# First modulation of a diffusion trunk by quarters of the channels, with the norm's squares summed on TensorE

## What is computed

```python
m = silu(c) @ ada_w + ada_b          # (6 * 1024,) for c, and again for c_ctx
sh1, sc1, g1, sh2, sc2, g2 = split(m, 6)
h = x * rsqrt(mean(x * x, channels) + 1e-6) * norm1_g
h = h * (1 + sc1) + sh1              # latents by c, context by c_ctx
q, i_in, gate, zf = h @ hg_w_in      # projections of the HGRN2 mixer
```

## Time and profile before

| what | us |
|---|---|
| median of 3 timed executions | 1887.09 |
| lowest and highest of them | 1884.05, 1888.6 |
| the profiled execution | 1884.44 |
| its span, first to last instruction | 1882.6 |
| TensorE busy in the span | 1794.5 |
| VectorE busy | 1160.9 |
| ScalarE busy | 676.3 |
| GpSimd busy | 79.3 |

### The profile page before, as it was taken

How to read it: one execution, slowest core, us unless ns; L and a number is a source line. 1 busy time by engine, 2 the same in 40 slices (tenths; PEclk the granted TensorE clock), 3 DMA queues, 4 the chain that set the end, 5 groups by cost and what they waited for, 6 DMA issues and landing times.

```text
span 1882.6 us, 31499 instructions
## 1 busy us (share of the span) xinstructions
PE 1794.5 (95%) x13510; PEld 1533.7 (81%) x13510; DVE 1160.9 (62%) x1921; ACT 676.3 (36%) x999; POOL 79.3 (4%) x146
## 2 busy tenths in 40 slices
PE   4999999999878999999999999999899999999997
PEld 4999999999766888888888888878655878888885
DVE  4467668666874676524564265576554598487485
ACT  4334333443222333312322133333776344233242
POOL 0000000000300000000000000000343000000000
PEclk9999999999988999999999999999999999999998
DMA  7221222112201033223332232222000222232222
GB/s 299 101 90 51 86 91 91 68 69 91 79 2 56 34 124 112 95 108 112 114 121 102 90 118 107 79 71 79 24 1 1 89 90 90 101 101 91 99 95 106
DMA packets 45801, 166.16 MB, mean 88 GB/s; under 512 B 4960, under 2 KB 5344, under 8 KB 45664
## 3 DMA queue, kind: packets, MB, share of 16 engines
q1 hardware_dynamic: 45664, 164.16, 24.4%
HBM read 162.05 MB, written 2.10 MB: 87 GB/s over the span
## 4 chain that ended last, share of the span: by engine, by line
PE 88%; DVE 7%; ACT 2%; issue 1%; DMA 1%; POOL 0%; DVEq 0%; SPq 0%; ACTq 0%
PE slot L437 31%; PE slot L426 9%; PE slot L428 8%; PE slot L427 8%; PE slot L884 4%; PE slot L886 4%; PE slot L885 4%; PE MB L494 2%; PE MA L886 2%; PE MA L884 2%; PE MA L885 2%; PE MA L598 2%; PE slot L837 2%; PE MB L804 1%; PE slot L814 1%
## 5 line engine op out<-in xcount | busy, mean ns | idle before, releaser
L1316 DVE TENSOR_TENSOR WL<-WR,WH 128x1024 fp32r<-128x1024 f32 x204 | 249.4, 1223 | 229.0 <-ACT WH L939 228.0
L939 ACT ACTIVATE WH<-WR 128x1024 fp32r<-128x1024 f32 x204 | 215.4, 1056 | 388.6 <-DMA WR<-in_w 388.6
L426 PE MATMUL slot<-HH,WH 128*128 128x384 f32 (+2 forms) x848 | 304.1, 359 | 16.8 <-DVE HL L1475 6.2
L428 PE MATMUL slot<-HH,WL 128*128 128x384 f32 (+2 forms) x848 | 293.8, 346 | 0.0
L427 PE MATMUL slot<-HL,WH 128*128 128x384 f32 (+2 forms) x848 | 293.6, 346 | 0.0
L437 PE MATMUL slot<-HH,WH 128*128 128x256 f32 (+1 forms) x816 | 212.2, 342 | 2.5 <-DVE ACC L1685 1.6
L437 PE MATMUL slot<-HH,WL 128*128 128x256 f32 (+1 forms) x816 | 210.1, 339 | 0.0
L437 PE MATMUL slot<-HL,WH 128*128 128x256 f32 (+1 forms) x816 | 207.7, 336 | 0.0
L426 PEld LDWEIGHTS slot<-HH,WH 128*128 128x128 f32 x848 | 161.3, 190 | 37.1 <-issue 10.3
L437 PEld LDWEIGHTS slot<-HH,WH 128*128 128x128 f32 x816 | 151.6, 189 | 25.8 <-issue 7.1
L437 PEld LDWEIGHTS slot<-HL,WH 128*128 128x128 f32 x816 | 153.8, 188 | 18.0
(11 more groups left out here) (234 smaller groups left out, 2950.5 us busy)
## 6 DMA issues: line engine op xcount, KB each, us to landing
WR<-in_w SPq DMA_DIRECT2D x204, 512.0 KB, 3.5
ada_raw<-in_ada SPq DMA_DIRECT2D x80, 512.0 KB, 4.6
AD<-in_ada SPq DMA_DIRECT2D x6, 1024.0 KB, 18.0
X<-in_x SPq DMA_DIRECT2D x4, 768.0 KB, 8.4
ada_raw<-in_ada SPq DMA_DIRECT2D x2, 1024.0 KB, 13.0
out<-Y SPq DMA_DIRECT2D x8, 256.0 KB, 2.2
Y<-in_masks SPq DMA_DIRECT2D x1, 512.0 KB, 17.7
rope<-in_rope SPq DMA_DIRECT2D x1, 512.0 KB, 3.8
```

Of the source, the lines that this page charges most:

```text
L426: mm(SLOT[s][:, po], WH[w % NB][:, k, :], hi[:, k, to], start=(k == 0), stop=False)
L428: last = mm(SLOT[s][:, po], WL[w % NB][:, k, :], hi[:, k, to], start=False, stop=(k == kn - 1))
L939: go(WH[t % NB][:, :, :], WR[t % NB][:, :, :], ACT.Copy).then_inc(w_hi_done, 1)
L1316: tt(WL[t % NB][:, :, :], WR[t % NB][:, :, :], WH[t % NB][:, :, :].bitcast(F32), ALU.subtract).then_inc(w_split, 1)
```

## The change

The first four groups are replaced by four quarters: quarter q holds the shift and the scale of channels 2q and 2q+1, 256 columns of each. Each quarter is loaded by four transfers of 512 KB, whose rows in memory are 256 values (1 KB) long instead of 1024 (4 KB). Weight tiles 0 and 1 come behind quarter 0, and tile 2 is issued ahead of the masks. `quarter(q)` on VectorE adds the bias and makes the coefficients of two channels at once.

The squares are no longer added on VectorE. ScalarE writes them to four buffers, and TensorE sums each channel's on arrival, 48 one-column products in all. The Sqrt table is brought in after channel 1's square. Fillers (`keep_busy`) are put ahead of the sums, between them, around the spread and around the first turn: 7, then 1 seven times, 3, 8, 1 and 7. TensorE's list has the quarters' products between the steps of the first two tiles. GpSimd makes the low half of weight tile 0, and VectorE that of tile 1 after waiting for it; VectorE made both before. ScalarE makes the high halves of both tiles between rows 0 and 1.

```diff
             for i in range(4):
                 sp.dma_start(X[:, 2 * i:2 * i + 2, :], x_in[:, 2 * i:2 * i + 2, :]).then_inc(x_in_done[i], 16)
-            for g in range(ADA_FIRST):
-                at = 4 * ADA_ORDER[g]
-                for k in (0, 2):
-                    dst = AR0[:, k:k + 2, :, :] if g == 0 else AD0[:, 4 * g - 4 + k:4 * g - 2 + k, :, :]
-                    sp.dma_start(dst, ada_in[at + k:at + k + 2].rearrange("n p (f o) -> p n f o", f=2)).then_inc(ada0_in[2 * g + k // 2], 16)
-                if g == 1:
+            for q in range(ADA_FIRST):
+                for f in range(2):
+                    g = 2 * f + q // 2
+                    at = (q % 2) * 256
+                    for k in range(2):
+                        cols = ada_in[4 * g:4 * g + 4].rearrange("n p o -> p n o")[:, :, 512 * k + at:512 * k + at + 256]
+                        sp.dma_start(first_weights(q)[:, f, :, k, :], cols).then_inc(ada0_in[q], 16)
+                if q == 0:
                     for t in range(2):
                         sp.dma_start(WR[t][:, :, :], w_in[t]).then_inc(w_in_done[t], 16)
+            sp.dma_start(WR[2][:, :, :], w_in[2]).then_inc(w_in_done[2], 16)
             sp.dma_start(mask_stage, masks_in).then_inc(masks_in_done, 16)
...
+            def weights_low(t):
+                pool.wait_ge(w_hi_done, t + 1)
+                pool.tensor_tensor(WL[t % NB][:, :, :], WR[t % NB][:, :, :], WH[t % NB][:, :, :].bitcast(F32), ALU.subtract).then_inc(w_split, 1)
+
+            weights_low(0)
             split_heads()
...
+            pe.wait_ge(small_in_done, 16)
+            pe.wait_ge(ident_in_done, 16)
+            REST = SLOT[1][:, 512:768]
+            keep_busy(7, REST)
             pe.wait_ge(silu_ready, 1)
...
-            square_sums(0)
+            squares.add(KC)
+            for k in range(KC):
+                pe.wait_ge(sq_ready, k + 1)
+                for c in range(NCH):
+                    last = mm(MA[:, c:c + 1], SQ4[k % 4][:, c * P:(c + 1) * P], ones[:, :], start=(k == 0 and c == 0), stop=(k == KC - 1 and c == NCH - 1))
+                last.then_inc(sq_summed if k < KC - 1 else ss_ready, 1)
+                if k < KC - 1:
+                    keep_busy(1, REST)
+            stats.add()
+            keep_busy(3, REST)
+            spread(0, MA)
+            keep_busy(8, REST)
             ada_first(0)
-            pe.wait_ge(ident_in_done, 16)
+            keep_busy(1, REST)
             ada_turn()
-            spread(0, MA)
-            ada_first(1)
-            ada_turn()
-            ada_first(2)
+            keep_busy(7, REST)
...
             first_steps(0)
+            ada_first(1)
+            first_steps(1, (0,))
             ada_turn()
-            first_steps(1)
+            first_steps(1, (1,))
+            ada_first(2)
+            first_steps(2, (0,))
+            ada_turn()
+            first_steps(2, (1,))
+            first_steps(3)
             ada_first(3)
-            first_steps(2)
+            first_steps(4, (0,))
             ada_turn()
-            for k in range(3, KC):
+            first_steps(4, (1,))
+            for k in range(5, KC):
                 first_steps(k)
...
-                square(c, slice(0, TOK))
-            added.add(KC - 2)
+                if c >= 4:
+                    act.wait_ge(sq_summed, c - 3)
+                go(SQ4[c % 4], X[:, c, :], ACT.Square).then_inc(sq_ready, 1)
+                if c == 1:
+                    go(sqrt_set[:, :], eps_t[:, :], ACT.Sqrt)
...
             row_copy(0)
+            split_high(1)
+            first_his(0, 2)
             row_copy(1)
-            split_high(1)
-            first_his(0, 1)
+            first_his(2, 3)
             row_copy(2)
-            first_his(1, 3)
+            first_his(3, 5)
             row_copy(3)
-            first_his(3, 4)
+            first_his(5, KC)
             split_high(2)
-            first_his(4, KC)
...
+            def first_low():
+                low.add()
+                dve.wait_ge(w_split, 1)
+                split_low(1)
...
-                coefs(0)
+                quarter(0)
                 dve.wait_ge(rstd_spread, stats.now())
                 scaled(0)
-                split_low(0)
                 scaled(1)
                 low(0)
-                split_low(1)
+                first_low()
+                low(1)
+                quarter(1)
                 scaled(2)
-                low(1)
...
```

More of the change, by code:

```diff
@@ L61 @@
 ADA_FIRST = 4
-ADA_ORDER = (0, 2, 1, 3)
 NB = 3
@@ L208, in trunk @@
         SSQ = Y[:, 2, :]
+        SQ4 = [Y[:, i, :] for i in (0, 1, 2, 5)]
         NT = [Y[:, 3, :], Y[:, 4, :]]
@@ L215, in trunk @@
         ident_in_done, masks_in_done = sem("ident_in_done"), sem("masks_in_done")
-        ada0_in = [sem(f"ada0_in{i}") for i in range(2 * ADA_FIRST)]
+        ada0_in = [sem(f"ada0_in{i}") for i in range(ADA_FIRST)]
         ada0_used = sem("ada0_used")
@@ L226, in trunk @@
         ada_copied, ada_turned, ada_ready = sem("ada_copied"), sem("ada_turned"), sem("ada_ready")
-        sq_ready, sq_added = sem("sq_ready"), sem("sq_added")
+        sq_ready, sq_added, sq_summed = sem("sq_ready"), sem("sq_added"), sem("sq_summed")
         ss_ready, std_ready = sem("ss_ready"), sem("std_ready")
@@ L253, in ada_row, with first_weights @@
             return row0 if n < ADA_FIRST else RB if n < ADA_FIRST + HEADS else row2
+        def first_weights(q):
+            part = AR0[:, :, :, :] if q == 0 else AD0[:, 4 * q - 4:4 * q, :, :]
+            return part.rearrange("p a b o -> p (a b o)").rearrange("p (f n k o) -> p f n k o", f=2, n=4, k=2)
         def of_level(t, at, tokens, s):
@@ L348, in load_piece @@
                 sp.dma_start(AR[i % 4][:, :, :], ada_in[n].rearrange("p (f o) -> p f o", f=2)).then_inc(piece_in[i % 4], 16)
-            for t in range(2, TILES):
-                if t >= NB:
-                    sp.wait_ge(tile_done, t - NB + 1)
+            for t in range(NB, TILES):
+                sp.wait_ge(tile_done, t - NB + 1)
                 sp.dma_start(WR[t % NB][:, :, :], w_in[t]).then_inc(w_in_done[t % NB], 16)
@@ L535, in spread, with keep_busy @@
                 last.then_inc(rstd_spread, 1)
-            def keep_busy(n):
+            def keep_busy(n, dst=MA[:, 512:768]):
                 for _ in range(n):
-                    mm(MA[:, 512:768], ident[:, :], small[:, 0:256], start=True, stop=True)
+                    mm(dst, ident[:, :], small[:, 0:256], start=True, stop=True)
             def norm_pe(first, more=True):
@@ L551, in norm_pe, with ada_first @@
                     keep_busy(7)
+            pe.wait_ge(small_in_done, 16)
+            pe.wait_ge(ident_in_done, 16)
+            REST = SLOT[1][:, 512:768]
+            keep_busy(7, REST)
             pe.wait_ge(silu_ready, 1)
[L554 to L559, removed]
+            def ada_first(q):
+                pe.wait_ge(ada0_in[q], 64)
+                for c in range(KC):
+                    for m in range(4):
+                        w = first_weights(q)[:, m // 2, c // 2, c % 2, (m % 2) * P:(m % 2) * P + P]
+                        last = mm(MB[32 * m:32 * m + 32, 0:P], silu_w[:, c, :], w, start=(c == 0), stop=(c == KC - 1))
                 last.then_inc(ada0_used, 1)
                 rows.add()
-            square_sums(0)
+            squares.add(KC)
[10 more added lines that the diff above has]
+            keep_busy(8, REST)
             ada_first(0)
-            pe.wait_ge(ident_in_done, 16)
+            keep_busy(1, REST)
             ada_turn()
-            spread(0, MA)
-            ada_first(1)
-            ada_turn()
-            ada_first(2)
+            keep_busy(7, REST)
             level, head, scored, mixed = Tally(), Tally(), Tally(), Tally()
@@ L698, in head_products, with first_steps @@
                         products(s, half, k, HH, HL)
-            def first_steps(k):
+            def first_steps(k, slots=(0, 1)):
                 pe.wait_ge(lo_ready, k + 1)
-                for s in range(2):
+                for s in slots:
                     if k == 0:
@@ L1376, in token_rstd, with quarter @@
                 nc.vector.reciprocal(rstd6[:, first:NCH], std6[:, first:NCH]).then_inc(rstd_ready, 1)
-            dve.wait_ge(ident_in_done, 16)
-            for c in range(KC):
-                add_square(c, TOK)
             token_rstd(0)
[L1382 to L1385, removed]
+            def first_low():
+                low.add()
+                dve.wait_ge(w_split, 1)
+                split_low(1)
             def first_norm():
                 squares.add(KC)
-                def coefs(a):
+                def quarter(q):
+                    rows.add()
+                    dve.wait_ge(ada_turned, rows.now())
+                    made = ada[:, 0:2 * KC, :].rearrange("p (f c) v -> p f c v", f=2)[:, :, 2 * q:2 * q + 2, :]
+                    bias = ada_b[:, 0:2 * KC].rearrange("p (f c) -> p f c", f=2)[:, :, 2 * q:2 * q + 2]
```

(29 more changed lines are left out.)

## The result

The changed kernel takes 1896.99 us (median of 4, 1895.87 to 1898.41) against 1886.67 (4 runs): a ratio of 1.0056, interval [1.0039, 1.0073]. The change made the kernel about 10 us slower, where 8 us of gain were forecast. The profiled execution is 1898.41 us.

A forecast was written before the change was run, and what follows sets the result against it. TensorE alone sets the time once the third tile begins; T at 41.5 plus 11.8 puts that at 53.3, not 61.4 us, 8.1 gained: profiled 1884.44 - 8.1 = 1876.3, median 1878.5 (1875 to 1881.5; 8 in 10, 1873.5 to 1886).

The forecast's parts named there:

- T: Start of quarter 3's products on TensorE, forecast at 40 to 41.6 us and taken as 41.5.
- a sum takes 0.11 at a later norm, a filler 0.22: TensorE's squares in the opening: these prices make a step 0.9 us at full clock, the last sum near 17.5.
- Rival A: Clock stays at 1.2 GHz through the opening's sums, which end at 22.5 us; gain only 2.6 us; chance 0.13.
- the end at full clock: Last of TensorE's sums at 17.5 us, against 22.5 at half clock, because of fillers ahead of and between them.
- Rival C: Loads in 1 KB pieces run at 192 GB/s, so the third tile begins 10.1 us later; chance 0.09.
- the line through two rows: Load rate estimated from the 4 KB and 2 KB piece rows: 51 ns for 1 KB, 330 GB/s.
- The page's rule: Skill's three cycles of overhead per piece: 1 KB loads at some 390 GB/s, quarter 3 landing near 36.5, not 41.5.
- the opening alone sets the time: Before 61.4 us lies all the change touches; behind it TensorE is busy 138.35 of 138.60 us and moves along unchanged.
- GpSimd's subtraction: Low half of weight 0 in the first step: 2.4 us taken, 4.25 at most, ending at 26.4 to 28.2.
- the first step's waits: VectorE waits for GpSimd in step 0; first slot opens at 27.2 us against 34.63, second at 28.4.
- The 1.4 us that I gave to a late load: TensorE's wait after step 1, from 33.8 us until quarter 2 is loaded at 35.2.
- the path from T: Quarter 3's products through step 7's first slot and ScalarE's reads, to the third tile's start: 11.8 us.

The follow-up runs named there:

- mid_fill_3: The changed kernel with three fillers instead of one behind each channel's sums; one run, 1894.01 us.
- hi_order: The changed kernel with ScalarE making channel 5's high half ahead of row copy 3; one run, 1893.85 us.
- best: The changed kernel with VectorE's adds, fillers moved (23 ahead of the sums) and channel 5's high half ahead of row copy 3; ratio to before 0.9980.
- best_wide: The kernel "best" with 4 KB rows in the loads instead of 1 KB; ratio to before 0.9985.
- no_fill: The changed kernel without any of its 28 fillers in the opening; ratio to before 1.0045.

## Why the prediction was wrong

The predicted and the measured time of each part of the way to the third tile (us):

| part | predicted | measured |
|---|---|---|
| to the last sum | 17.5 | 33.2 |
| fillers, root and spread, to quarter 0's products | 3.1 | 7.5 |
| to the first projection | 6.6 | 6.7 |
| to quarter 3's products (T) | 14.3 | 14.2 |
| from T to the third tile | 11.8 | 13.4 |

**The step that failed** is "a sum takes 0.11 at a later norm, a filler 0.22". The rows count two instructions to a sum or filler and I divided by instructions, then multiplied by the code's calls. A step is 1.78 us and not 0.9, and TensorE, taken to follow ScalarE closely, became the bound. That alone, at full clock, moves the last sum to 23.6 and the fillers and spread behind it to 5.4 us (11 fillers at 0.43, 0.7 for the spread); the rest as measured would give 29.0 + 6.7 + 27.6 = 63.3: no gain but a loss of 2. It was in reach: the second norm makes 6 calls, and x12 stands in the earlier trace rows.

**Rival A was the other half.** It had the clock stay low from the start; in fact the fillers ran at half speed up to about 10 us, the first two sets of sums at full speed, and the clock fell at 13.2, in a stretch with no idle time. It had the price of a sum wrong by the same factor of two, and so a gain of 2.6 where the right price gives a loss. The forecast took the end at full clock (17.5 and not 22.5) because of the fillers, and that was its second fault: 9.6 us. The Trainium skill (TensorE: Matmul & The Clock Gate, "HAM oscillation — how this bites in real kernels") warns of idle gaps; here the fall came without one, and with three fillers between the sums (mid_fill_3) there was none.

**Rival C**, the only one on the slower side, was wrong: its 10.1 us match the outcome by accident. The pieces of 1 KB ran at 349 GB/s at a share of 1.09, which is 320 at a full one; the line through two rows gave 330 at 1.03, which is 320 too. Quarter 3 was in by about 41, as estimated, and needed at 61.6. The page's rule, which gave 390 GB/s, does not agree with this row, and the row decides.

**Right:** that the opening alone sets the time (the tail was the same within 3 us in all traces); GpSimd's subtraction, 2.37 us against 2.4; the first step's waits; and, by luck, the path from step 0 to T: no load was awaited there. The 1.4 us that I gave to a late load were in fact an idle 1.03 us ahead of channel 2's step, for its low half, which I had left out, and some 0.3 us of longer steps.

**Left out of the account:** from the first projection to the third tile the changed kernel takes 27.6 us and the kernel before took 26.8. Three sets of products, 1.95 us each, now stand in that stretch and one ahead of it; before it was one in it and three ahead. What the quarters save lies ahead of the first projection: 6.7 us from the first products to it, against 12.6 before.

**Too small by 1.6 us:** the path from T. VectorE could not add quarter 3 at T + 3.3, because ahead of it in its list stood channel 5's low half, whose high half stood behind row copy 3 on ScalarE. Rows of ScalarE, then VectorE, in the changed kernel:

```profile
63.59 0.28 ACT L1137 ACTIVATE row<-MB 128x128 f32<-128x128 f32 x1 [2.34 <-PE MB L577]
63.76 1.11 ACT L1144 ACTIVATE HH<-Y,ada 128x256 fp32r<-128x256 f32 x2
```

```profile
64.91 1.15 DVE L1450 SCALAR_TENSOR_TENSOR HL<-Y,ada,HH 128x256 fp32r<-128x256 f32 x2 [2.48 <-ACT HH L1144]
65.97 0.16 DVE L1433 TENSOR_TENSOR ada<-MB,small 128x8 f32<-128x8 f32 x1
```

The add came at T + 4.4 and channel 6's step at T + 8.3, where 7.0 was forecast; hi_order, with the exchange, has that step at T + 7.3 and took back 1.0 us. The last 0.3 us of the 1.6 are in the steps behind it (5.1 us to the third tile, not 4.8).

## What to carry to other kernels

Before pricing a new operation from a merged row, divide the row's count by the calls in the code: a full-precision matmul stands there twice. Moving a sum from a vector engine to TensorE as one-column products trades 0.96 us an add for 1.28 us at best and 2.56 at half clock, and the clock can fall among such products without an idle gap. Put fillers first in a gap that is idle anyway, directly ahead of the work that needs the clock. Between ready work and its consumer each is a price that must be won back by the clock: none between the sums ended them at 25.8 us, three at 29.8, one at 33.2. On a path of several engines check what a waiting copy holds up behind it.

## What the runs showed of the hardware

TensorE's clock fell from 2.4 to 1.2 GHz at 13.2 us in the changed kernel while the engine was busy without a break (12 one-column and 2 wide instructions in turn), and held from 10.07 to 29.78 us, in one execution, through the same sums with 6 wide instructions between. It fell in some executions and not in others of nearly the same TensorE list (1.00 against 0.67 in 20 to 30 us in "best" and best_wide). The profile's clock column reads 1.00 until its first change, also over one-column products that took 0.215 us each and not 0.107 (no_fill, 9.19 to 29.80 us). Loads of 1 KB pieces alone in a full queue ran at 345 to 351 GB/s in windows of 2 us (changed kernel and "best", 22 to 36 us), 4 KB pieces at 401 to 422 (before and best_wide, 14 to 36 us).
